# Block 1 in two groups of 256 tokens, with the second dealt out among the expert slots of the first

## The reference, cut to what matters

```python
def first_block(x, c, ...):
    shift1, scale1, gate1, shift2, scale2, gate2 = silu(c) @ w_ada + b_ada          # 6 x 1024
    hn = modulate(rmsnorm(x, norm1_g), shift1, scale1)
    qa, ka, va, qi, ki, wi, qb, kb, vb, ga, gb = split(hn @ w_in)
    ya = dsa_attention(qa, ka, va, qi, ki, wi, rel_bias)      # top 128 of the causal keys, softmax
    yb = stick_breaking_attention(qb, kb, vb)                 # 8 heads of 64
    merged = sigmoid(ga) * (ya @ w_proj_a) + sigmoid(gb) * (yb @ w_proj_b)
    x = x + gate1 * (merged @ w_out)
    hn2 = modulate(rmsnorm(x, norm2_g), shift2, scale2)
    return rmsnorm(x + gate2 * peer_ffn(hn2, ...), final_g)

def peer_ffn(h, w_q, sub_keys, u, v):
    s = einsum('thcd,hcnd->thcn', (h @ w_q), sub_keys)        # 8 heads, 2 halves, 128 keys each
    eidx, g = the 16 best of the sums of the 16 best of each half, and their softmax
    pre = einsum('td,thkd->thk', h, u[eidx])                  # 128 experts of 1024 a token
    return einsum('thk,thkd->td', g * gelu(pre), v[eidx])
```

## Time and profile before

| | us |
|---|---|
| median of 3 runs (2405.41 to 2417.39) | 2416.7 |
| span of the profiled execution, first to last instruction | 2407.7 |
| PE, DVE, ACT, POOL busy in it | 1877.5, 1439.3, 988.3, 574.0 |

### The profile page before, as it was taken

The page is one execution under the profiler, slowest core; times in us unless marked ns, Lnnn a source line. Parts: engine busy times, 40 slices in busy tenths (PEclk is TensorE's granted clock), DMA queues, the critical chain, the costliest instruction groups (busy, mean ns, idle before and its releaser), DMA issues.

```text
span 2407.7 us, 37910 instructions
## 1 busy us (share of the span) xinstructions
PE 1877.5 (78%) x14736; PEld 1182.7 (49%) x14736; DVE 1439.3 (60%) x3280; ACT 988.3 (41%) x2352; POOL 574.0 (24%) x554
## 2 busy tenths in 40 slices
PE   5998889999766644444435798988888885999999
PEld 3877457777333311100002453355666553677887
DVE  6747744554877677777777768765444333223554
ACT  3123545523443333333333576844444212343443
POOL 0000000001444444444344334443333331000000
PEclk8999999999887655555556897689999997999999
DMA  8932002233999999999999999999999996313565
GB/s 298 333 98 71 1 29 68 71 108 136 404 419 420 420 420 420 420 420 418 418 417 400 405 411 409 390 418 418 418 417 417 418 418 266 118 54 110 184 182 168
DMA packets 123616, 712.12 MB, mean 296 GB/s; under 512 B 14592, under 2 KB 15744, under 8 KB 57648
## 3 DMA queue, kind: packets, MB, share of 16 engines
q0 software_dynamic: 74608, 542.25, 54.6%
q1 hardware_dynamic: 48592, 167.33, 19.9%
q10 hardware_dynamic: 240, 0.16, 0.0%
HBM read 707.56 MB, written 2.13 MB: 295 GB/s over the span
## 4 chain that ended last, share of the span: by engine, by line
PE 46%; DMA 31%; DVE 10%; ACT 6%; issue 5%; POOL 2%; ACTq 0%; SPq 0%; DVEq 0%
DMA arena<-experts,eidx 30%; PE psum L718 9%; PE psum L719 8%; PE psum L720 8%; PE psum L1017 7%; DVE arena L1975 5%; POOL arena L1945 2%; PE psum L1308 2%; PE psum L1135 2%; ACT arena L1589 1%; PE psum L1185 1%; PE psum L1223 1%; ACT sq L1597 1%; PE psum L1259 1%; PE psum L1062 1%
## 5 line engine op out<-in xcount | busy, mean ns | idle before, releaser
L1975 DVE CUSTOM_DVE_ANT_0 arena<-arena 128x1024 f32<-128x1024 f32 x560 | 679.5, 1223 | 412.0 <-DMA arena<-experts,eidx 371.0
L1017 PE MATMUL psum<-arena,sq 32*32 32x512 f32 x8192 | 445.4, 842 | 449.4 <-ACT sq L1597 340.7
L1945 POOL DMA_INDIRECT arena<-experts,eidx x512 | 560.8, 1095 | 947.6 <-PE psum L1017 778.5
L1017 PEld LDWEIGHTS psum<-arena,sq 32*32 32x32 f32 x8192 | 95.1, 120 | 694.6 <-ACT sq L1597 500.5
L1583 ACT ACTIVATE arena<-arena 128x2 f32<-128x2 f32 x256 | 52.0, 203 | 736.5 <-DVE arena L1975 722.1
L718 PE MATMUL psum<-hn_high,w_high 128*128 128x512 f32 (+1 forms) x416 | 176.2, 424 | 15.4 <-DVE hn_low L1972 15.4
L720 PE MATMUL psum<-hn_high,ring_low 128*128 128x512 f32 (+1 forms) x432 | 175.2, 405 | 0.0
L719 PE MATMUL psum<-hn_low,w_high 128*128 128x512 f32 (+1 forms) x416 | 170.4, 410 | 0.0
L1330 PE MATMUL psum<-n_t,ring 128*128 128x256 f32 x704 | 164.3, 389 | 1.1 <-DVE n_t L1972 1.1
L1330 PEld LDWEIGHTS psum<-n_t,ring 128*128 128x128 f32 x704 | 132.5, 192 | 48.7 <-issue 30.1
L1597 ACT ACTIVATE sq<-sq,arena 128x32 f32<-128x32 f32 x512 | 136.9, 313 | 23.8
(11 more groups left out here) (327 smaller groups left out, 3102.1 us busy)
## 6 DMA issues: line engine op xcount, KB each, us to landing
ring<-w_stream SPq DMA_DIRECT2D x262, 512.0 KB
arena<-w_ada SPq DMA_DIRECT2D x48, 512.0 KB, 6.3
arena<-experts,eidx POOLq DMA_INDIRECT x512
arena<-cum_rows POOLq DMA_DIRECT2D x1, 2112.0 KB, 9.7
x<-xT SPq DMA_DIRECT2D x1, 2048.0 KB, 12.6
arena<-rel_rows POOLq DMA_DIRECT2D x1, 2048.0 KB, 15.3
arena<-sub_keys POOLq DMA_DIRECT2D x1, 1024.0 KB, 5.8
outT<-hn_rest SPq DMA_DIRECT2D x8, 128.0 KB
```

What stands on the lines that cost most here:

```text
L1017: last = mm(bank(4 + 2 * odd + a)[QUART * b:QUART * b + QUART, :], diag[k, s, :], rows[k, s, D + a * 512:D + (a + 1) * 512], start=c == 0, ...
L1945: nc.gpsimd.indirect_dma_start(rows[:, s, :], None, experts, bass.IndirectOffsetOnAxis(ap=eidx[:, n // P % 2, n % P:n % P + 1], axis=0)).t ...
L1975: return V.tensor_tensor_reduce(out=out, in0=a, in1=b, scale=1.0, scalar=0.0 if op1 == ALU.add else -TAKEN, op0=op0, op1=op1, accum_out=accum)
```

## The change

1. Block 1 runs for tokens 0 to 255 alone ahead of the slots, with the same three products, of 256 columns now. Keys and values are also stored to DRAM. ACT, not DVE, moves queries and keys out of the banks.
2. The gathers start when the first heads of tokens 0 to 127 are chosen. `late_block` holds block 1 for tokens 256 to 511, cut into 251 ticks: one for each slot up to 127, nine for eight slots from then on, so it ends about slot 237. Its 78 weight tiles are loaded a second time, are not split, and are multiplied in plain fp32. Stick breaking goes head by head over all keys (ticks 42 to 90), DSA attention in 8 steps (100 to 136), gates and projections from 138, output from 186, the experts' queries from 212. Keys and values of the first tokens are loaded back from DRAM.
3. PE's share of a slot's late work stands ahead of the slot's `combine`; on ACT it stands behind `diagonals`, on DVE behind `dots` and `choose`.
4. The choices of experts are spread evenly, one head in 16 slots.
5. `block2(0)` keeps its ticks from slot 276 on, and `block2(1)` its place; buffers and banks are laid out anew.

```diff
+L_MEAN, L_ROOT, L_KI, L_WI, L_QI, L_IDX = 1, 6, 10, 14, 18, 21
+L_TOP = 39
+L_B, L_BH = 42, 6
+L_A, L_AS = 100, 4
+L_G, L_GM = 138, 6
+L_O = L_G + L_GM * KT
+L_N2 = L_O + 2 * KT + 4
+L_Q = L_N2 + 6
...
+def ring_order():
+    queries = [(4 * (j - LEAD), 0, S_WQ + j) for j in range(LEAD, 2 * PH)]
+    both = sorted(queries + [(t, 1, tile) for t, tile in L_DENSE])
+    return [(0, tile) for tile in range(S_WQ + LEAD)] + [(g, tile) for _, g, tile in both]
...
+def late_ticks(n):
+    return 1 + (n >= P and n % 8 == 0)
...
 def choose_plan():
-        elif todo and (n // PK >= EARLY or n % PK < PARTS or n < PK + PARTS // 2):
-            at[n].append(todo.pop(0))
+    for c in range(FIRST + 1, HEADS):
+        for p in range(PARTS):
+            at[PK * (c - 1) - 9 + p].append((c, p))
...
+            def late_dense(n):
+                r, b = LATE_AT[n], late_bank(n)
+                if not S_GATE + KT <= n < S_PROJ:
+                    claim(b, "dense", n)
+                pe.wait_ge(ring_ready[r % SLOTS], 16 * (r // SLOTS + 1))
+                w = ring[:, r % SLOTS, :].rearrange("p (k m) -> p k m", m=P)
...
+                        last = mm(bank(b, PAIR, half), w[:, k, :], rhs[:, k, :], start=k == 0, stop=k == KT - 1)
+                last.then_inc(tile_done.sem, 1)
...
+            def late_block():                                  # PE
+                for t in range(L_END):
+                    if t in LATE_TILE:
+                        late_dense(LATE_TILE[t])
+                    for shift, f in ((6, late_weighted), (3, late_sums), (0, late_z)):
+                        h = due(t, L_B + shift, L_BH, NH)
+                        if h is not None:
+                            f(h)
+                    for shift, f in ((8, late_values), (6, late_transposes), (0, late_scores)):
+                        st = due(t, L_A + shift, L_AS, 2 * HP)
+                        if st is not None:
+                            f(st)
+                    yield
...
             for n in range(HEADS * PK):                        # PE
+                for _ in range(late_ticks(n) if n < PAIR else 0):
+                    next(late, None)
                 if n % 2 == 0:
                     combine(n)
...
+            def late_soft(h):                                  # ACT
+                a = late_az[h % 2]
+                late_filled(act, "z", h, 2)
+                late_filled(act, "z", h, 3)
+                act.preload_act_table_set("natural_log_exp_and_others")
+                steps(op(a, sticks, ACT.Abs))
+                steps(op(a, a, ACT.Exp, scale=-1.0))
+                op(a, a, ACT.Ln, bias=1.0).then_inc(l_soft.sem, 1)
```

More of the change, by code:

```diff
@@ L347, in program @@
[L347 to L379, removed]
-        late = {i: take(2, T - P * i) for i in (1, 0)}
@@ L381, in program @@
-        assert used[0] <= gates_at + 16 * T
-        def sp_of(p, i):
-            return early[i][p % 2] if i >= 2 else late[i]
-        used[0] = 0
-        sc = take(TT, 16, NK)
-        h_tok_at = used[0]
-        h_tok = take(TT, D)
-        rows_at = used[0]
-        rows = take(SLOT, 2 * D)
-        small_at = used[0]
-        used[0] = h_tok_at + D
-        keys = take(16, NK)
-        qh = [take(T) for _ in range(2)]
-        used[0] = small_at
-        spare = over("spare", [P, 2 * D], "hn_high", f32)
@@ L831, in z_pair @@
                 for e in range(2):
[L832 removed]
+                    last = z_product(step, e, True)
+                last.then_inc(z_done.sem, 1)
             def sums(step):
[L835 to L837 removed]
+                p, i = step // 2, 1 - step % 2
@@ new lines, in early_keys, with early_rows, late_rows @@
+            def early_keys(j):
+                late_emptied(pe, "early query", j)
+                claim(0, "key", j)
+                fill(key_products(j, 0, j), 0, "key", j)
+            def early_rows(a):
+                claim(0, "rows", 1, a)
+                fill(split_rows(1, range(4 * a, 4 * a + 4), lambda k: bank(0, P, k % 4 * P)), 0, "rows", 1, a)
+            def late_rows(n, a):
+                claim(2 + a, "rows", n, a)
+                for k in range(4 * a, 4 * a + 4):
+                    last = nc.tensor.transpose(bank(2 + a, P, k % 4 * P), n1[:, k, (n - 2) * P:(n - 1) * P], ident[:])
+                fill(last, 2 + a, "rows", n, a)
@@ L1114, in last_rows @@
                                 last.then_inc(act_turned.sem, 1)
+                if g == 0:
+                    yield from ticks.until(3)
+                    for b in range(4):
+                        pe.wait_ge(late_free[b], late_uses[b])
                 for t in range(2):
@@ new lines, in late_weights, with late_y_out @@
+            def late_weights(h):
+                a = late_az[h % 2]
+                for b, first, last in ((2, 0, 3 * P), (3, 3 * P, 7 * P)):
+                    late_filled(act, "u", h, b)
+                    emptied(op(a[:, first:last], sticks[:, first:last], ACT.Exp), "z", h, b)
+            def late_y_out(e, p):
+                if e:
+                    late_filled(act, "yb", p, 1)
+                else:
+                    late_filled(act, "pv", p, 3)
+                emptied(op(late_y[e][:, p, :], bank(0, PAIR), ACT.Copy), *(("yb", p) if e else ("pv", p)))
@@ L2541, in block2 @@
                     dve.sem_inc(bank_free[b], 1)
-                yield from ticks.until(T_END)
             low(S_WQ + 2)
```

1499 lines of the change are left out of this document (982 added, 517 removed).

## The result

| | us |
|---|---|
| before, median of 20 runs (2402.41 to 2419.63) | 2411.6 |
| after, median of 20 runs (2417.86 to 2455.96) | 2424.6 |
| ratio, 95% interval | 1.0062 [1.0044, 1.0080] |
| span of the profiled execution after | 2419.9 |

The account below looks back on a forecast made before the run. PE was taken to bound the stages before the first gather and the last part, the DMA the slots between. 2407.7 - 257 + 108 + 20 = 2278.7 us of span, 2288 us as median; range 2235 to 2370 us.

Parts of the forecast that it names:

- Term 1: Stages before the slots: with half the tokens the first gather comes at 330 instead of 587.1 us, 257 us less (200 to 276).
- The rival that the split sets the early pace: Early dense tiles: the split on ACT and DVE sets the pace, term 1 gains only 200, total 2345 us; chance 0.13.
- Term 2: Slots with the DMA full: 45.1 MB of added loads at 418 GB/s are paid in full, 108 us.
- Term 3: The 237 slots with late work: engines have room, so it adds only 20 us to the pace, bounds 0 and 74.
- 6 us of slack absorb a head's burst, such as a softplus that waits for ACT.: Late slots: a gather could be issued some 6 us later before the DMA ran dry, covering delays ahead of a combine.
- No engine is over its share: Over 716 us of late slots PE needs 73%, DVE 80% and ACT 61%, so all have room.
- paid one engine behind the other: Late slots: nothing of a slot pair overlaps, 5.0 us a slot, 469 us instead of 20, 2737 us in all; chance 0.07.
- The price of PE's work: Late slots: a plain fp32 matmul of 256 columns takes 0.231 us, PE needs 524 of 716 us in all.
- Half clock as the pace of the late slots: Late slots: PE at a granted clock of 0.50 sets the pace, term 3 becomes 74, 2342 us; chance 0.16.
- Table loads: Attention slots: if each ACT table load cost twice 1.28 us, ACT is the bound, 34 us more, 2322 us; chance 0.04.

Follow-up runs that it names:

- e2: Changed kernel with ACT emptying a late dense tile's bank one tick behind the tile instead of two: 2377.3 us, 0.9874 of before.
- e6: e2 with a head of stick breaking every eight slots instead of six, more ticks between its hand-offs, later parts moved back 16 ticks: 2339.6 us, 0.9708 of before.
- e4: Changed kernel with half of each late dense tile's matmuls left out, all loads and evacuations kept: 2419.8 us, 1.0003 of before.
- e5: e2 and e4 together, the earlier evacuation with half of each late dense tile's matmuls left out: 2357.1 us, 0.9793 of before.
- e10: e6 with half of each late dense tile's matmuls left out, as in e4: 2331.2 us, 0.9654 of before.
- e3: Changed kernel with late Ln, Exp, Abs and Tanh replaced by Copy or Identity, preloads gone, late output not added to x: 2393.0 us, 0.9931 of before.
- e12: e6 with the late block's ACT functions replaced by Copy and Identity and late output not added to x, as in e3: 2318.3 us, 0.9649 of before.
- e11: e6 with ACT's evacuation of an early query tile one slot earlier: 2350.3 us, 0.9749 of before.
- e8: e6 with DVE taking a DSA step's logits two ticks behind PE's scores instead of one: 2351.7 us, 0.9756 of before, one run at 5101.9 us.

## Why the prediction was wrong

**Term 1, the first gather: mechanism right, 231 us of the 257, inside its bounds of 200 to 276.** The stages ended at about 110, 140, 175 and 258 us where I had 111, 142, 176 and 251. The projections and the output then took to 330 us: 72 instead of 57 us. From 300 to 330 us PE was busy 29.4 of 30, so they still went at PE's pace of products, not at DVE's; I had counted too few of these (the 72 us hold 522 records of matmuls, 16 tiles of 24 are 384). The rival that the split sets the early pace (2345 us) is out.

**Term 2, the bytes: right.** The kernel moves 758.5 MB instead of 712.1, 46.4 more where I had 45.1. Where the DMA is full it goes at 417 to 418 GB/s, and slots 144 to 239 take 3.05 to 3.18 us for my 3.02.

**Term 3, the pace of the late slots: +132 us instead of +20, far above my bound of 74. This is the step that failed**, in two places.

*"6 us of slack absorb a head's burst, such as a softplus that waits for ACT."* They do not, since what stands in line adds up: from the end of PE's products to the next combine ACT has 7.8 us (574.37 to 582.15: 4.2 us of softplus with its table load, 2.4 us for the diagonals behind it with theirs, and the hand-overs), and the tile by tokens in its single bank held PE for another 7.9. A head then takes 26.5 us, and six slots at 3.02 us are 18.1. One head every eight slots (24.2 us) comes near it, and with e2 slots 0 to 239 fall from 857.8 to 767.3 us, 11 of which come back behind slot 240.

"No engine is over its share" hid the second half. My 73, 80 and 61% are averages over 237 slots, and they say what each engine does, not in which order it may do it. The densest stretch, slots 48 to 95, holds 24 combines of 1.07 us, six tiles of 3.65, three of 3.74 and eight heads of 9.3: some 133 us of PE at full clock (an estimate from the rows), of the 145 that 48 slots take at 3.02. That is 92%, with no wait in it; in e6 the same sum is 115 us, 79%. I had named the right mechanism in the rival "paid one engine behind the other", priced it at 2737 us as if nothing overlapped, and rejected it. It came true in part: 857.8/240 = 3.57 us a slot, just short of the 3.65 from which I had said it would decide; with the 26 us missing in term 1 it sufficed. What I had against it, eight row buffers, lets DVE run ahead, but it does not take ACT's softplus from in front of the diagonals.

*The price of PE's work.* I took 29.55/128 = 0.231 us for a plain fp32 matmul of 256 columns. The profile shows that such a matmul leaves two records, so the 128 in the earlier trace rows are 64 matmuls, and one takes 0.46 us: L1167 has 976 records for 61 tiles of 8 matmuls, and one tile is 16 records and 3.72 us, not 1.85. A tile by tokens takes 3.74 us at full clock, not 3, and up to 6.67 behind a stop. My 127 and 27 us are 257 and 34 (49 as they ran). In turn the combine, 1.09 us a slot at a clock of 0.50, is half that at full clock (2.25 us a pair in the earlier trace rows, 1.14 for the one at 604.79 us above), so the 258 us are about 128. A head's small matmuls take 9.3 us in the chain (5.8 from 621.25 us and 3.5 from 628.10), not 5.2. So 524 us becomes some 565 of 716, 79%: the total still fits, the densest stretch hardly. The halved tiles (e4, e5, e10) show what half of the tiles costs in time: 27 to 30 us in slots 0 to 239, and 29 to 33 in slots 32 to 143, where some 50 us of work were removed.

**The other rivals.** Half clock as the pace of the late slots (2342 us) is out: PE was granted 0.85 in the worst stretch. It came in another form, behind each stop: if each row of PE in slots 32 to 143 is weighted with the clock granted in it, its 343 busy us are 294 at full clock, so about 50 us of PE's time there went to the low clock (an estimate from the trace; how much of it lies on the path no run shows). Table loads: the next activation starts 0.01 to 0.02 us behind the load of 1.28 us, as in the earlier trace rows, so the price that I had given this rival is not there; the Trainium skill ("ScalarE: Activation LUTs", What ACT_TABLE_LOAD costs) has a drain of about 1380 ns besides, and the trace again does not show it. And ACT was busy only 49%. Still, without them the time falls by 32 us (e3) and 21 us (e12 against e6). The chain has them between PE's products and the next combine (1.28 us twice in the 7.8 above), so they cost time though ACT is not full; my sum had counted them in ACT's share, at no price.

**What stays open.** Slots 16 to 47 take 3.6 to 3.9 us in e6 too, of which the half tiles remove 0.7 in 32 to 47. Slots 128 to 143 take 4.03 us in e6, where the moved DSA steps end. e11 did not gain, and the 5101.9 us run of e8 has no explanation. The clock of 0.50 before the slots came in some executions and not in others. That the diagonals behind ACT's softplus are what holds up PE was read from the chain; no run moved them ahead of it. Nor does a run separate the distance of the hand-offs from the number of heads per slot.

**The best version** is e6: 2339.6 us, 2.9% under the kernel before and 3.5% under the changed one, by edits of the order alone.

## What to carry to other kernels

When work is dealt out among the steps of a loop that runs on several in-order engines, write down the turn of one piece through the engines, with what stands in each queue behind each of its waits, and compare it with the time of the steps that the piece is given: here 26.5 us a head against 18.1 us for six slots. Take the shares of busy time over the densest stretch and not over the whole (92% here, where the average at the right prices is 79). Spread the pieces until a turn fits, and free a single buffer as early as its reader can: two such edits were worth 85 us here, halving TensorE's dense work 20 to 30. Before a price is taken from counted records, check what one instruction of the code leaves in the profile.

## What the runs showed of the hardware

A plain fp32 matmul is two records of MATMUL, an fp32r one a single record: 256 columns cost 0.46 us in plain fp32 and 0.118 us from start to start in one split product at a clock of 1.00, so on TensorE the three products of the split together (0.35 us) are cheaper than one plain fp32 matmul; the split has its price on ACT and DVE, 1.05 and 1.22 us a tile.

The same code was granted different clocks from 160 to 210 us: 0.97 to 1.00 in eleven of the profiled executions with the changed order of work, 0.50 and 0.56 in two (e4 and e10), and each of these two had its first gather 26 to 28 us later (381.92 us for 356.13, 384.5 for 356.8). At 0.50 the engine was busy all of the 50 us, at 0.97 for 47.2; the edit of both stands behind this stretch, and e5, which has it too, was granted 0.98. What decides it is not known.

The combine follows the clock (2.17 us a pair at 582.15 us, granted 0.50, and 1.14 at 604.79, granted 1.00, in the kernel after), so its cost in a stretch at 0.50 is twice what it is at full clock. The low clock came behind waits of PE: the combine at 582.15 follows 5.67 us of standing still, the tile at 613.79 7.86 us.
